# The gate's position bias as one-row matmuls into PSUM instead of a vector add

## The reference

```python
def chunked_spatial_gating(xc, ln_g, ln_b, w_s, b_s):
    z = jax.nn.gelu(xc)
    u, v = jnp.split(z, 2, axis=-1)
    v = layernorm(v, ln_g, ln_b).reshape(B, L // CHUNK, CHUNK, N_GMLP_HEADS, GMLP_HEAD_DIM)
    g = jnp.einsum('bnpec,eqp->bnqec', v, w_s) + b_s.T[:, :, None]
    return u * g.reshape(B, L, D_GMLP)

def first_block(...):
    h = rmsnorm(x, norm_mix[i])
    p = h @ w_in[i]
    y_a = multiscale_pool_mixer(p[..., :a_end], ...)
    y_b = hyena_mixer(p[..., a_end:b_end], ...)
    y_c = chunked_spatial_gating(p[..., b_end:], ...)
    x = x + jnp.concatenate([y_a, y_b, y_c], axis=-1) @ w_out[i]
    ...                       # feed-forward block, then a second layer
```

## Time and profile before

| | |
|---|---|
| median of 3 runs | 2527.4 us (2523.7 to 2529.11) |
| the profiled execution | 2523.7 us, of which the span in the trace is 2522.0 us |
| TensorE busy | 2439.0 us, 97% of the span |
| VectorE busy | 1535.3 us, 61% |
| ScalarE busy | 1185.3 us, 47% |
| share of the last-ending chain on TensorE | 91% |
| position mixing with the pool matmuls | from 261.26 to 265.47 us of the span |

### The profile page before, as it was taken

How to read it: one execution, slowest core, us unless ns; L and a number is a source line. 1 busy time by engine, 2 the same in 40 slices (tenths; PEclk the granted TensorE clock), 3 DMA queues, 4 the chain that set the end, 5 groups by cost and what they waited for, 6 DMA issues and landing times.

```text
span 2522.0 us, 51086 instructions
## 1 busy us (share of the span) xinstructions
PE 2439.0 (97%) x19936; PEld 2403.2 (95%) x19936; DVE 1535.3 (61%) x2056; ACT 1185.3 (47%) x1502; POOL 12.8 (1%) x27
## 2 busy tenths in 40 slices
PE   6999989999999999996999999999999999999999
PEld 6899989999999999996899999999999999999999
DVE  6556766666556666566866666766576454545454
ACT  5343435666435665434444444544465443433433
POOL 0000000000000000000000000000000000000000
PEclk9999999999999999998999999999999999999999
DMA  6453554555555555553333333333445355555554
GB/s 236 140 177 116 169 173 142 190 176 187 187 186 166 184 182 177 193 189 129 121 117 111 111 104 121 124 110 111 141 154 175 117 193 177 184 177 178 184 187 158
DMA packets 110193, 400.78 MB, mean 159 GB/s; under 512 B 12378, under 2 KB 12405, under 8 KB 109952
## 3 DMA queue, kind: packets, MB, share of 16 engines
q1 hardware_dynamic: 108000, 391.00, 46.5%
q0 software_dynamic: 2080, 8.06, 1.0%
HBM read 396.91 MB, written 2.10 MB: 158 GB/s over the span
## 4 chain that ended last, share of the span: by engine, by line
PE 91%; DVE 5%; issue 1%; ACT 1%; DMA 0%; DVEq 0%; SPq 0%; ACTq 0%
PE bank L419 91%; DVE w_lo L1317 1%; DVE scratch L1366 1%; ACT w_hi L910 1%; PE bank L612 1%; DVE h_lo L1363 0%; DVE s_k L1366 0%; DMA x<-in_xT 0%; DVE cum L1363 0%; DVE root L1405 0%; DVE ping L1363 0%; DVE s_t L1363 0%; DVE qr L1812 0%; DVE acc L1363 0%; DVE s_k L1363 0%
## 5 line engine op out<-in xcount | busy, mean ns | idle before, releaser
L1317 DVE TENSOR_TENSOR w_lo<-raw,w_hi 128x1024 fp32r<-128x1024 f32 x736 | 891.3, 1224 | 799.2 <-ACT w_hi L910 793.0
L910 ACT ACTIVATE w_hi<-raw 128x1024 fp32r<-128x1024 f32 x736 | 770.4, 1057 | 1011.5 <-PE bank L419 992.3
L419 PE MATMUL bank<-h_hi,w_hi 128*128 128x256 f32 x4016 | 1162.7, 290 | 36.8 <-DVE h_lo L1363 15.0
L419 PE MATMUL bank<-h_lo,w_hi 128*128 128x256 f32 x4016 | 1140.4, 284 | 0.0
L419 PE MATMUL bank<-h_hi,w_lo 128*128 128x256 f32 x4016 | 1140.3, 284 | 0.0
L419 PEld LDWEIGHTS bank<-h_hi,w_hi 128*128 128x128 f32 x4016 | 774.9, 193 | 47.3 <-issue 24.3
L419 PEld LDWEIGHTS bank<-h_lo,w_hi 128*128 128x128 f32 x4016 | 775.2, 193 | 3.2 <-issue 2.2
L419 PEld LDWEIGHTS bank<-h_hi,w_lo 128*128 128x128 f32 x4016 | 774.4, 193 | 0.0
L419 PE MATMUL bank<-m_hi,w_lo 128*128 128x256 f32 x704 | 197.8, 281 | 0.0
L419 PE MATMUL bank<-m_hi,w_hi 128*128 128x256 f32 x704 | 197.1, 280 | 0.0
L419 PE MATMUL bank<-m_lo,w_hi 128*128 128x256 f32 x704 | 195.7, 278 | 0.0
(11 more groups left out here) (413 smaller groups left out, 2795.8 us busy)
## 6 DMA issues: line engine op xcount, KB each, us to landing
raw<-in_units SPq DMA_DIRECT2D x736, 512.0 KB, 3.4
x<-in_xT SPq DMA_DIRECT2D x4, 512.0 KB, 5.7
memx<-in_memT POOLq DMA_DIRECT2D x4, 512.0 KB, 7.6
out_y<-obuf SPq DMA_DIRECT2D x8, 256.0 KB, 4.2
bias_t<-in_bias POOLq DMA_DIRECT2D x8, 192.0 KB, 2.9
dft<-in_dft POOLq DMA_DIRECT2D x1, 1024.0 KB, 7.6
decay<-in_decay POOLq DMA_DIRECT2D x1, 768.0 KB, 5.7
con<-in_con SPq DMA_DIRECT2D x1, 546.0 KB, 8.0
```

The lines of the kernel that those rows point to most:

```text
L419: return pe.matmul(out, lhsT, rhs, start=start, stop=stop, skip_group_check=True)
L910: return act.activation(out, in_, ACT.Copy, scale=scale)
L1317: dve.tensor_tensor(w_lo[slot][:, :, :], raw[slot][:, :, :], w_hi[slot][:, :, :].bitcast(F32), ALU.subtract).then_inc(split_done, 1)
```

## The change

The tile `bs` becomes one row on partition 0 (1x768), loaded without broadcast. Behind each of the 12 position-mixing matmuls comes another one that adds the bias into the same 128x128 place of PSUM: its stationary operand is the first row of `ones` (1x128), its moving operand the head's 128 bias values (1x128). VectorE's two additions of `bs` in `gated` and the wait for them go; the multiplication by `gu` now reads the bank.

```diff
-        bs = place("bs", [P, HY, P], 99 * K)
+        bs = place("bs", [1, HY * P], 99 * K)
...
-            for dst, src in ((ws[:, :, :], "ws"), (pw[:, :, :], "pw")):
+            for dst, src in ((ws[:, :, :], "ws"), (pw[:, :, :], "pw"), (bs[:, :], "bs")):
                 pool.dma_start(dst, a[src]).then_inc(mixer_in, 16)
-            pool.dma_start(bs[:, :, :].rearrange("p e q -> p (e q)"), a["bs"].broadcast_to([P, HY * P]))\
-                .then_inc(mixer_in, 16)
...
                     o = banks[3 + e // 2][:, (e % 2) * T + c * P:(e % 2) * T + (c + 1) * P]
-                    m = mm(o, gvt[:, c, e * P:(e + 1) * P], ws[:, e, :])
+                    mm(o, gvt[:, c, e * P:(e + 1) * P], ws[:, e, :], True, False)
+                    m = mm(o, con[0:1, CC["ones"][0]:CC["ones"][0] + P], bs[0:1, e * P:(e + 1) * P], False, True)
...
             def gated(k, last=None):
                 s = 2 * (k % 2)
-                for i in range(2):
-                    step(tt(y_part[:, s + i, :].rearrange("p (c q) -> p c q", c=2),
-                            banks[3 + k][:, i * T:(i + 1) * T].rearrange("p (c q) -> p c q", c=2),
-                            bcast(bs[:, 2 * k + i, :], 2), ALU.add))
-                settle()
-                to_act(tt(y_part[:, s:s + 2, :], y_part[:, s:s + 2, :], gu[:, 2 * k:2 * k + 2, :], ALU.mult))
+                to_act(tt(y_part[:, s:s + 2, :], gu[:, 2 * k:2 * k + 2, :],
+                          banks[3 + k][:, :].rearrange("p (s t) -> p s t", s=2), ALU.mult))
```

## The result

The changed kernel takes 2539.0 us in the median (2537.5 to 2541.0), against 2527.3 before. The ratio of the runs is 1.0054, with a 95% interval of 1.0039 to 1.0068: 10 to 17 us slower, 13.6 in the middle. Forecast were 2534.8 us, which is 7.4 us more. The direction was right, the size about half; run again beside the experiments, the changed kernel gave 1.0052 (1.0039 to 1.0066).

A forecast was written before the change was run, and what follows sets the result against it. The prediction took an unbroken TensorE chain as the bound: 4.8 us of round trips plus 2.6 us of stream, with VectorE's saving and the load at 0, gave 2527.4 + 7.4 = 2534.8 us, range 2529.5 to 2540.

The forecast's parts named there:

- What bounds: Around the mixing, an unbroken TensorE piece of 117.89 us bounds; every us TensorE gains or loses there moves the end.
- VectorE's part and the load: In the mixing stage, VectorE's 2.4 us of dropped additions and the broadcast load of `bs` are hidden: worth 0.
- The stream of the new matmuls: In the position mixing, 24 new TensorE instructions at 0.111 us each stream for 2.67 us, with nothing hiding them.
- The round trip between full and partial matmuls: In the mixing, each way into and out of a one-row matmul costs 0.40 us, twelve times: 4.8 us.
- the upper bound: Rival at the mixing's row changes: each waits for full latency, 0.275 us, +9.2 us in all; chance 0.09.
- The clock: In the mixing stage, the granted clock was expected to stay 1.00, so the sum holds no clock loss.
- The rival: Clock falls in the mixing stage and next full group as TensorE streams 5.2 of some 10 us: 2537 to 2542; chance 0.07.
- The sum: For the mixing stage, 4.8 us of round trips plus 2.6 us of stream make 7.4 us more.
- What is late next: After the mixing, the pool result comes some 7.4 us later, but no new TensorE wait; the tail only shifts.
- The lead: VectorE's first split for the output projection is ready ahead of TensorE's need; lead grows from 1.1 to about 6 us.

The follow-up runs named there:

- all-rows kernel: Changed kernel with the 12 bias matmuls on all 128 rows, zeros below the bias row; piece 120.57 us, ratio 1.0004.
- the block: Changed kernel with the 12 one-row matmuls together behind the 12 mixing matmuls; piece 120.96 us, ratio 1.0010.
- the spread: Changed kernel with one-row matmuls placed singly, one behind every 6 instructions of the group before; piece 125.11 us, ratio 1.0038.
- 64-row kernel: Changed kernel, each alternating bias matmul on 64 rows, zeros below the first; piece 125.21 us, ratio 1.0033.
- the long block: Changed kernel with the one-row matmuls together and four times over, 96 instructions without a gap; piece 137.10 us, ratio 1.0048.
- filled: Kernel before the change, second four 64-row filter-stage matmuls moved behind the next group's first unit; 2521.9 us, ratio 0.9983.
- once-a-head kernel: Changed kernel with one one-row matmul of 256 columns a head, 6 instead of 12; piece 125.99 us, ratio 1.0034.
- the shift: Kernel before the change plus 48 tiny, unused matmuls at its start, moving later TensorE instructions; 2520.3 us, ratio 0.9969.

## Why the prediction was right and where it was wrong

**What bounds.** Right. The chain's piece took the whole loss, and VectorE's part and the load measured 0 (0.9997, piece unchanged).

**The stream of the new matmuls.** Right: 2.68 us in the all-rows kernel, 2.67 forecast.

**The round trip between full and partial matmuls.** Right, and the nearest row was the 64-row one, as chosen: 0.40 forecast; 0.39 in the block, (7.22 - 2.68) / 12 = 0.38 in the spread, (7.32 - 2.68) / 12 = 0.39 with 64 rows. That is 0.19 to 0.20 for each change; the upper bound, 0.275, was not reached. Writing the same place of PSUM made no difference: 0.39 alternating into one place, 0.38 spread in a stream that writes another bank. The Trainium skill's "Mode switching requires drain" ("TensorEngine Tiling (Array Packing)", Tiling Modes, Key Properties) fits these gaps; the 166 ns that the page "TensorE: Matmul & The Clock Gate" gives for the fixed part of a lone bf16 matmul (Single matmul latency) is more than the gap on the way in, 254.50 to 254.71 instead of 0.12, so 0.09 us.

**The clock.** This is the step that failed. The prediction listed the fall with a chance of 0.07 and set it aside because "over the 64-row groups the clock was 1.00" and "no gap of the new stage is longer than 0.3 us". The first is true of the earlier trace rows at 1179 us only. In the filter stage of the same trace a group of 64-row matmuls ran in part at half the clock:

```profile
61.02 2.84 PE L419 MATMUL bank<-fw,fh 64*128 64x384 f32 x8
65.71 3.80 PE L419 MATMUL bank<-fw,fh 64*128 64x384 f32 x8 [1.85 <-DVE f_fwd L1363]
```

The first group took 2.84 us, the same work behind the idle time 3.80, and the clock was 0.74 over 65.7 to 69.4 us and 0.50 from 68 to 72; the prediction priced this stage by the full group behind alone. The second remark is true. Neither bears on one-row matmuls. The fall is worth 13.35 - 7.32 = 6.0 us, the changed kernel's piece less the 64-row kernel's, which has the same gaps at full clock. It is made of pairs that went from 0.84 to 1.45 us, and of the pool matmuls behind, full ones, which ran from 277.71 to 280.93 at 1.2 GHz, 3.2 us instead of the 1.5 between the same starts in the earlier trace rows. The rival also had the cause at best by half: it blamed the share of the time in which TensorE streams. The runs show one-row matmuls, close together, in its place: the long block streamed without a pause and its clock fell; the 64-row kernel had the gaps and its clock did not. That its total of 2537 to 2542 holds the measured time is in part luck. It put 5.2 us on the stage's own stream and 2.1 on the full group behind. In the trace seven slow pairs took 10.1 us instead of 5.8, so 4.2; the pool matmuls with the first full one lost 1.8 against the 64-row kernel (281.45 - 277.71 against 273.16 - 271.21), and the full group after them nothing.

The page "TensorE: Matmul & The Clock Gate" of the Trainium skill (Part 1, What's actually happening) lets the clock follow how busy TensorE has been. The filter stage agrees: filled, its clock stayed at 1.00. The long one-row block does not, if busy means issuing: its clock went to 0.53 without a pause.

**The sum.** 7.4 where 13.35 stands in the piece; at full clock 7.3. The term that was put at nothing is the clock's 6.0. The range's upper end, 2540, just held the median of 2539.0, but the ratio of 1.0054 on 2527.4 gives 2541, beyond it.

**What is late next.** No new wait on TensorE, as forecast, though VectorE's waits were longer, 7.39 us for the pool result. The lead grew as forecast: the first split for the output projection is done at 287.21 us and TensorE's first instruction on `y_hi` starts at 292.84, 5.6 us later, against 1.1 before.

What stays open: how few rows are few enough. One row brought the clock down in the changed kernel, the once-a-head kernel and the long block; 12 one-row matmuls in a block of 2.9 us or spread did not, nor did 64 rows. Nothing between 1 and 64 rows was run. The queue's rows don't name an engine; that the packets which went are TensorE's is inferred, from the shift being an edit of TensorE's program alone and from where the stalls were. Why a shift by this amount takes the stalls away was not worked out, and no other amount at the start of the kernel was tried.

## What to carry to other kernels

On a TensorE-bound path, a vector operation that hides behind TensorE is free, and moving it into a matmul is not: here 2.4 hidden us became 13. If a bias has to go in by matmul, put the one-row matmuls behind each other (3.1 us here) or fill the rows with zeros (2.7 us), but don't alternate them with full ones. And where the clock falls, look for idle rows as well as for idle time; TensorE's busy time does not show the idle rows.

## What the runs showed of the hardware that was not expected

- One-row matmuls can halve TensorE's clock without any pause: 96 in a row, clock 1.00 over the first 3.7 us and 0.53 over the next 13; on 128 rows 1.00 throughout.
- A matmul between full ones costs the same 0.6 us with 1 row as with 64: at full clock the alternating pairs lie 0.83 us apart in both kernels, of which the full matmul is 0.22.
- Moving TensorE's code by 48 matmuls, of which none does useful work, made the unchanged kernel 7.5 us faster, about as much as the change in question costs at full clock. The page "Runtime: NRT & Kernel Launch" of the Trainium skill (Instruction fetch mechanics) says that instructions are fetched in 16 KiB blocks and that a taken branch to a block that is not at hand waits for it. The trace agrees in kind: 1.59 MB in 97 packets is 16.4 KB each, and they fell to 71 when the stalls went.
